# Expert stage of a hybrid block on one core: the banks are emptied by ScalarE, the expert loads move one job, the row buffers become four

## The chip, the core and the metric

The kernel runs on one core of one Trainium2 chip. The time is device microseconds of one execution, from the first to the last instruction on the core with what lies around them; less is better. PE is TensorE, ACT is ScalarE, DVE is VectorE, POOL is GpSimd, SP is SyncE, which here only issues transfers.

## The reference

One block of an encoder over 512 tokens of width 2048, all in float32. The change touches the last part of it, an expert layer (`peer`) with 128 x 128 = 16384 single-neuron experts, of which each token picks 8 x 16 = 128:

```python
def one_block(args):
    xb, eb, gb = args                      # tokens, experts picked, gates
    a = jnp.einsum("td,thkd->thk", xb, u[eb])
    act = gb * jax.nn.gelu(a)
    return jnp.einsum("thk,thkd->td", act, v[eb])
x = x + gate2 * peer(h2, ...)
```

## The kernel before

Tokens are split. 352 of them (`TD`) go through all experts densely: the U stage multiplies them with all 16384 rows of `u` (128 jobs, one 1 MB weight block each), writes the gelu of the result to memory (`gelu_scratch`), and builds the gates as a dense table (`gate_scratch`). The V stage multiplies gate times gelu with all of `v`, again 128 jobs of 1 MB. The other 160 tokens go by rows: POOL fetches for each pick the picked row of 128 tokens at once (an indirect transfer of 128 rows of 8 KB, 1 MB), and DVE takes the dot products (128 + 32 of them, `dot` and `dot_x`) and later adds the gated rows of `v` to `y_g` and `y_x` (128 + 32, `v_step`). The last 24 of `dot_x` and all of `v_step` lie in the V stage: 12 rows for every 8 jobs.

A weight job takes the same way in both stages, with two buffers at each step. SP loads `w_raw` for job n as soon as DVE is done with job n-2. ACT rounds it to `w_hi` (`hi`) once it is loaded and PE has finished job n-2. DVE subtracts to get `w_lo` (`lo`). PE multiplies 48 times (16 pieces, three products each).

In the V stage the left operand comes from `load_unit`: SP loads 4 experts of gelu (`wt`, 0.72 MB) and their gates (`gate_l`, 0.72 MB, in pieces of 512 bytes); DVE multiplies them (`weigh`), ACT rounds (`weigh_hi`), DVE subtracts (`weigh_lo`), one such unit for four jobs; PE needs it some six jobs later. `wt` and `gate_l` have one buffer each.

PE's sums of 8 jobs (a segment, 4 jobs for the first) stay in the eight PSUM banks. Then `add` scales them and adds them to `acc_o` on DVE, bank by bank, and the next segment's first matmul in a bank waits for its `added`.

The order on each engine is written out by hand in loops of 16 slots r; slot r treats weight job 6 + r (and 16 more in each turn). Slots r and r + 8 have the same form but for the half of the result, so 8 jobs are called a period here, with slots 0 to 7. SP in slot r issues the load of job 8 + r:

```python
with sp.Fori(0, 7) as i:
    for r in range(16):
        load_v(8 + r, i)
        if r % 4 == 2:
            load_unit(4 + r // 4, i)
```

DVE in slot r: `add` if r % 8 == 7, `lo`, `weigh` if r % 4 == 0, a row, `weigh_lo` if r % 4 == 1, a second row if r is even. ACT in slot r: `hi`, and behind it `weigh_hi` if r % 4 == 0. All three work strictly in order.

Of the kernel before, what the change touches and what calls it, by code (L numbers as in the profile page):

```python
# [13 lines left out]
P = 128  # L14
# [80 lines left out]
def build(nc, x_d, c_d, pos_d, prm_d, wada_d, win_d, wqr_d, wval_d, whd_d, wout_d, wwq_d, keys_d, u_d, v_d, urow_d, vrow_d, out_d):  # L95
    gelu_d = nc.dram_tensor("gelu_scratch", [NKEY, P, TD], F32).ap()
# [3 lines left out]
    with ExitStack() as ctx:  # L100
# [77 lines left out]
        e1_g = at("e1_g", 182, [P, P])  # L178
        e2_g = at("e2_g", 182.5, [P, P])
        part_g = at("part_g", 183, [P, P], U32)  # L180
        shifted_g = at("shifted_g", 183.5, [P, PH_, TOPK])
        expd_g = at("expd_g", 184, [P, PH_, TOPK])
        esum_g = at("esum_g", 184.5, [P, PH_])
        ersum_g = at("ersum_g", 184.75, [P, PH_])
        row_f = at("row_f", 185.5, [P, P])
# [9 lines left out]
        g_chunk = [at(f"g_chunk{s}", 112 + 24 * s, [P, NKEY, GC]) for s in range(2)]  # L195
        u_row = [at(f"u_row{s}", (160, 168, 192)[s], [P, D]) for s in range(3)]
        h2t = at("h2t", 0, [P, KD, T])[:, :, T - P:T]
        h2x = at("h2x", 32, [P, KD, T])[:, :, T - P:T]
        x_keep = at("x_keep", 208, [P, KD, XT])
        x_rep = at("x_rep", 192, [P, KD, P // XT, XT])  # L200
        hot2 = at("hot2", 176, [P, 2, 4, P, 2], BF16)
        hot1 = [at(f"hot1{j}", 180 + 4 * j, [P, 2, 4, P, 2], BF16) for j in range(3)]
# [7 lines left out]
        wt_hi = [at(f"wt_hi{s}", 112 + 6 * s, [P, 4, TD], F32R) for s in range(4)]  # L210
        wt_lo = [at(f"wt_lo{s}", 136 + 6 * s, [P, 4, TD], F32R) for s in range(4)]
        wt = at("wt", 176, [P, 4, TD])
        gate_l = at("gate_l", 182, [P, TD // GC, 4, GC])
# [60 lines left out]
        seg_sum, added = sem("seg_sum"), sem("added")  # L274
# [18 lines left out]
        def _(sp):  # L293
# [98 lines left out]
        def _(pool):  # L392
# [1487 lines left out]
```

## Time and profile before

| | |
|---|---|
| median of 3 runs | 3391.32 us (3388.0 to 3401.11) |
| profiled execution | 3383.77 us, span 3381.9 us |
| busy: PE / DVE / ACT / POOL | 91% / 79% / 31% / 21% |
| mean granted TensorE clock | 0.953 |
| transfers | 892.73 MB, 264 GB/s over the span |

The U stage's loop runs from about 1203 to 2200 us of the span, the V stage from 2239 us to the end. Busy shares are means over stages; a matmul's duration overlaps with its neighbour's, so a busy PE can still be slow. The granted clock is the share of 2.4 GHz (0.5 is 1.2 GHz).

### The profile page before, as it was taken

To read this page: it belongs to the slowest core of one execution; us is meant where nothing else is said; L and a number is where in the kernel's file an instruction comes from. 1 tells how busy PE (TensorE), PEld (TensorE's weight loads), DVE (VectorE), ACT (ScalarE), POOL (GpSimd) and SP (SyncE) were. 2 spreads that over 40 slices of the span, in tenths; PEclk is the share of its full clock that TensorE was granted. 3 is DMA by queue.
4 is the path that set the end of the run, shared out by engine and by line. 5 is a ranking of instruction groups with operands and counts; after the bars stand their busy time and mean duration, and the time that the engine had idled before them with its cause. 6 is when DMAs were issued, how large, how long until landed. Compare 5 with 4: busy or idle time off the path is not lost.

```text
span 3381.9 us, 44834 instructions
## 1 busy us (share of the span) xinstructions
PE 3070.1 (91%) x17253; PEld 2798.5 (83%) x17253; DVE 2673.7 (79%) x3081; ACT 1043.0 (31%) x992; POOL 724.3 (21%) x380
## 2 busy tenths in 40 slices
PE   4898978879889989999899999978999889998899
PEld 3686744447678989999899999978999889998899
DVE  6996968867773699999789999857887877877875
ACT  3323233431122334444333333222222222222221
POOL 4500000000030013233112323322332322323231
PEclk8998989879999999999999999989999999999999
DMA  8621213237734357777569999988899888898985
GB/s 349 253 100 62 83 55 128 115 122 303 292 152 174 136 195 296 298 297 297 215 219 371 357 366 371 376 333 320 334 349 343 325 347 331 339 352 315 356 336 199
DMA packets 194324, 892.73 MB, mean 264 GB/s; under 512 B 15664, under 2 KB 93616, under 8 KB 98096
## 3 DMA queue, kind: packets, MB, share of 16 engines
q1 hardware_dynamic: 123664, 491.29, 38.6%
q0 software_dynamic: 46080, 335.56, 25.8%
q10 hardware_dynamic: 24480, 64.45, 4.9%
q8 instruction: 74, 1.21, 0.1%
q14 instruction: 26, 0.21, 0.0%
HBM read 836.71 MB, written 54.53 MB: 264 GB/s over the span
## 4 chain that ended last, share of the span: by engine, by line
PE 56%; DVE 17%; DMA 17%; issue 4%; ACT 3%; POOL 2%; SPq 1%; DVEq 0%; ACTq 0%; POOLq 0%; PEldq 0%
PE bank L1459 11%; PE bank L1460 11%; PE bank L1461 11%; DMA gate_l<-gate_scratch 9%; PE bank L1793 4%; PE bank L1794 4%; PE bank L1795 4%; DMA u_row<-v_rows,urow_i 4%; DVE w_lo L830 3%; PE bank L1767 2%; ACT w_hi L452 2%; DVE ada_w L855 2%; PE bank L1670 2%; PE bank L1671 2%; PE bank L1672 2%
## 5 line engine op out<-in xcount | busy, mean ns | idle before, releaser
L452 ACT ACTIVATE w_hi<-w_raw 128x2048 fp32r<-128x2048 f32 (+1 forms) x327 | 620.2, 1897 | 1455.1 <-PE bank L1461 526.4
L830 DVE TENSOR_TENSOR w_lo<-w_raw,w_hi 128x2048 fp32r<-128x2048 f32 (+1 forms) x319 | 727.3, 2280 | 406.8 <-ACT w_hi L452 388.5
L1459 PE MATMUL bank<-act_hi,w_hi 128*128 128x352 f32 (+1 forms) x2584 | 886.9, 343 | 59.6 <-DVE w_lo L830 44.1
L1460 PE MATMUL bank<-act_lo,w_hi 128*128 128x352 f32 (+1 forms) x2584 | 877.2, 339 | 0.0
L1461 PE MATMUL bank<-act_hi,w_lo 128*128 128x352 f32 (+1 forms) x2584 | 876.5, 339 | 0.0
L1793 PE MATMUL bank<-wt_hi,w_hi 128*128 128x352 f32 x2048 | 682.2, 333 | 106.8 <-DVE acc_o L1384 65.2
L1794 PE MATMUL bank<-wt_lo,w_hi 128*128 128x352 f32 x2048 | 676.4, 330 | 0.0
L1795 PE MATMUL bank<-wt_hi,w_lo 128*128 128x352 f32 x2048 | 675.7, 330 | 0.0
L1459 PEld LDWEIGHTS bank<-act_hi,w_hi 128*128 128x128 f32 x2584 | 491.7, 190 | 94.1 <-issue 38.3
L1461 PEld LDWEIGHTS bank<-act_hi,w_lo 128*128 128x128 f32 x2584 | 491.4, 190 | 22.3
L1460 PEld LDWEIGHTS bank<-act_lo,w_hi 128*128 128x128 f32 x2584 | 492.4, 191 | 20.9 <-issue 0.2
L1793 PEld LDWEIGHTS bank<-wt_hi,w_hi 128*128 128x128 f32 x2048 | 399.5, 195 | 116.1 <-issue 69.5
L432 POOL DMA_INDIRECT u_row<-u_rows,urow_i x128 | 260.4, 2034 | 932.8 <-DVE u_row L1229 648.2
L1794 PEld LDWEIGHTS bank<-wt_lo,w_hi 128*128 128x128 f32 x2048 | 400.0, 195 | 0.0
L1795 PEld LDWEIGHTS bank<-wt_hi,w_lo 128*128 128x128 f32 x2048 | 399.0, 195 | 0.0
L432 POOL DMA_INDIRECT u_row<-v_rows,urow_i x128 | 228.4, 1784 | 519.9 <-DVE y_g L1374 505.9
L1374 DVE SCALAR_TENSOR_TENSOR y_g<-u_row,gate_g,y_g 128x2048 f32<-128x2048 f32 x128 | 300.4, 2347 | 33.5 <-DMA u_row<-v_rows,urow_i 30.7
L1229 DVE SCALAR_TENSOR_TENSOR u_row<-u_row,h2t 128x2048 f32<-128x2048 f32 x128 | 288.7, 2284 | 10.2 <-DMA u_row<-u_rows,urow_i 10.1
L421 POOL TENSOR_TENSOR act_lo<-X,act_hi 128x512 fp32r<-128x512 f32 x16 | 26.6, 1679 | 791.6 <-ACT act_hi L467 791.6
L1501 PE MATMUL bank<-act_hi,w_hi 128*128 128x512 f32 x256 | 105.1, 411 | 56.1 <-POOL act_lo L409 27.1
L1343 DVE TENSOR_TENSOR wt<-wt,gate_l 128x1408 f32<-128x1408 f32 x32 | 51.9, 1622 | 89.8 <-DMA gate_l<-gate_scratch 89.8
L1670 PE MATMUL bank<-act_hi,w_hi 128*128 128x512 f32 x256 | 107.0, 418 | 5.6 <-DVE act_lo L1116 2.9
(262 smaller groups left out, 3323.7 us busy)
## 6 DMA issues: line engine op xcount, KB each, us to landing
w_raw<-u SPq DMA_DIRECT2D x128, 1024.0 KB
w_raw<-v SPq DMA_DIRECT2D x128, 1024.0 KB
ada_w<-wada SPq DMA_DIRECT2D x80, 1024.0 KB, 5.6
w_raw<-win SPq DMA_DIRECT2D x27, 1024.0 KB
gelu_scratch<-gelu_s ACTq DMA_DIRECT2D x128, 176.0 KB
gate_scratch<-g_chunk ACTq DMA_DIRECT2D x11, 2048.0 KB, 14.2
wt<-gelu_scratch SPq DMA_DIRECT2D x32, 704.0 KB
gate_l<-gate_scratch SPq DMA_DIRECT2D x32, 704.0 KB
```

The lines of the kernel that those rows point to most:

```text
L432: pool.indirect_dma_start(u_row[n % 3][:], None, table, bass.IndirectOffsetOnAxis(ap=col, axis=0)).then_inc(u_row_loaded[n % 3], 16)
L452: act.activation(w_hi[n0 % 2][:, 0:width], w_raw[n0 % 2][:, 0:width], ACT.Copy).then_inc(hi_done, 1)
L830: dve.tensor_tensor(w_lo[s][:, 0:width], w_raw[s][:, 0:width], w_hi[s][:, 0:width].bitcast(F32), ALU.subtract).then_inc(lo_done, 1)
L1229: dve.scalar_tensor_tensor(out=row, in0=row, scalar=1.0, in1=h2t, op0=ALU.mult, op1=ALU.mult, accum_out=col).then_inc(dots_done, 1)
L1374: dve.scalar_tensor_tensor(out=y[:], in0=u_row[s % 3][:], scalar=col, in1=y[:], op0=ALU.mult, op1=ALU.add).then_inc(y_g_steps, 1)
L1459: pe.matmul(out, wh, hi_t(k), start=(k == 0), stop=False)
L1460: pe.matmul(out, wh, lo_t(k), start=False, stop=False)
L1461: last = pe.matmul(out, wl, hi_t(k), start=False, stop=(k == nk - 1))
L1670: pe.matmul(bank[s][:], wh, act_hi[:, k, :], start=(at_ == 0), stop=False)
L1793: pe.matmul(o, w_hi[s][:, col], th, start=begin is not None and e == 0, stop=False)
L1794: pe.matmul(o, w_hi[s][:, col], tl, start=False, stop=False)
L1795: last = pe.matmul(o, w_lo[s][:, col], th, start=False, stop=bool(end) and e == 1)
```

## The change

Five edits, all in or for the V stage:

1. ACT empties the banks: `evict` scales a bank into one of eight SBUF tiles `stage`; PE's next segment waits for `evicted`. DVE's `add` becomes a sum of two SBUF tiles, four in slot 0 and four in slot 1 of the next slots.
2. `load_unit` is issued at r % 4 == 1 and not 2; it still waits for the `weigh_lo` of the unit before.
3. `weigh` stands behind the two rows of its slot and not ahead of them.
4. Rows in the V stage (24 of `dot_x` and all `v_step`) use four buffers `v_row`, not three; the first waits until the first 8 of `dot_x` are done.
5. `gelu_scratch` is laid out by partition, so that `wt` is 5632 contiguous bytes per partition and not four pieces of 1408.

Buffers move to make room, `h2x` becomes contiguous, and `y_g` is cleared in the V stage's third job.

```diff
-    gelu_d = nc.dram_tensor("gelu_scratch", [NKEY, P, TD], F32).ap()
+    gelu_d = nc.dram_tensor("gelu_scratch", [P, NKEY, TD], F32).ap()
...
-                sp.dma_start(wt[:], gelu_d[rows].rearrange("e p t -> p e t")).then_inc(wt_loaded, 16)
+                sp.dma_start(wt[:], gelu_d[:, rows, :]).then_inc(wt_loaded, 16)
...
                     load_v(8 + r, i)
-                    if r % 4 == 2:
+                    if r % 4 == 1:
                         load_unit(4 + r // 4, i)
...
+                elif n >= XT - 4:
+                    pool.wait_ge(y_g_steps, m - 2)
...
+            def evict(k, half_i, turn=0):
+                for d in range(8):
+                    act.wait_ge(seg_sum, 8 * k + d + 1 + turn * 16)
+                    if k:
+                        act.wait_ge(added, 8 * (k - 1) + d + 1 + turn * 16)
+                    m = 5 * KD + 8 * half_i + d
+                    act.activation(stage[d][:], bank[d][:, 0:TD], ACT.Copy, scale=mod[:, m:m + 1]).then_inc(evicted, 1)
...
                 for r in range(16):
+                    if r % 8 == 7:
+                        evict(1 + r // 8, 1 - r // 8, i)
                     hi(J_V + 6 + r, i * 8)
                     if r % 4 == 0:
                         weigh_hi(3 + r // 4, i)
...
                 for r in range(16):
-                    if r % 8 == 7:
-                        add(1 + 2 * i0 + r // 8, 1 - r // 8, turn)
                     lo(J_V + 6 + 16 * i0 + r, turn * 8)
-                    if r % 4 == 0:
-                        weigh(3 + 4 * i0 + r // 4, turn)
+                    if r % 8 < 2:
+                        add(2 * i0 + r // 8, r // 8, r % 8, turn)
                     row(q)
                     if r % 4 == 1:
                         weigh_lo(3 + 4 * i0 + r // 4, turn)
                     if r % 2 == 0:
                         row(q + 1)
+                    if r % 4 == 0:
+                        weigh(3 + 4 * i0 + r // 4, turn)
...
-                opened = () if q == 0 else (y_ready, 1) if q == 124 else (added, 8 * (segment - 1) + 1) if r == 0 else None
+                opened = () if q == 0 else (y_ready, 1) if q == 124 else (evicted, 8 * (segment - 1) + 1) if r == 0 else None
```

SP's queue in the V loop before, from the load in slot 1 to that in slot 3 (`w_raw_54` and `w_raw_55` are the two weight buffers, and a name's number is a buffer's):

```order
L298 DMA w_raw_54<-v 128x2048
...
L298 DMA w_raw_55<-v 128x2048
...
L360 DMA wt<-gelu_scratch 128x4x352
...
L361 DMA gate_l<-gate_scratch 128x11x128
...
L298 DMA w_raw_54<-v 128x2048
```

The same place now:

```order
L301 DMA w_raw_54<-v 128x2048
...
L363 DMA wt<-gelu_scratch 128x1408
...
L364 DMA gate_l<-gate_scratch 128x11x128
...
L301 DMA w_raw_55<-v 128x2048
...
L301 DMA w_raw_54<-v 128x2048
```

The unit's two transfers have moved ahead of the load issued in slot 2, which is the weight block for slot 4 (or slot 0 of the next period).

DVE before, from the last `lo` ahead of a `weigh` through the slot after it (slots 0 and 1):

```order
L830 TENSOR_TENSOR w_lo_59<-w_raw_55,w_hi_57 128x2048
...
L1343 TENSOR_TENSOR wt<-wt,gate_l 128x1408
...
L1374 SCALAR_TENSOR_TENSOR y_g<-u_row_159,gate_g,y_g 128x2048
...
L1374 SCALAR_TENSOR_TENSOR y_g<-u_row_160,gate_g,y_g 128x2048
...
L830 TENSOR_TENSOR w_lo_58<-w_raw_54,w_hi_56 128x2048
...
L1374 SCALAR_TENSOR_TENSOR y_g<-u_row_161,gate_g,y_g 128x2048
...
L1347 TENSOR_TENSOR wt_lo_184<-wt,wt_hi_180 128x1408
```

Slots 0 and 1 now, without the second and third of four adds in each:

```order
L847 TENSOR_TENSOR w_lo_59<-w_raw_55,w_hi_57 128x2048
...
L1399 TENSOR_TENSOR acc_o<-acc_o,stage_193 128x352
...
L1399 TENSOR_TENSOR acc_o<-acc_o,stage_196 128x352
...
L1392 SCALAR_TENSOR_TENSOR y_g<-u_row_159,gate_g,y_g 128x2048
...
L1392 SCALAR_TENSOR_TENSOR y_g<-u_row_160,gate_g,y_g 128x2048
...
L1363 TENSOR_TENSOR wt<-wt,gate_l 128x1408
...
L847 TENSOR_TENSOR w_lo_58<-w_raw_54,w_hi_56 128x2048
...
L1399 TENSOR_TENSOR acc_o<-acc_o,stage_197 128x352
...
L1399 TENSOR_TENSOR acc_o<-acc_o,stage_200 128x352
...
L1392 SCALAR_TENSOR_TENSOR y_g<-u_row_161,gate_g,y_g 128x2048
...
L1367 TENSOR_TENSOR wt_lo_184<-wt,wt_hi_180 128x1408
```

Between the `lo` and the `weigh` of a slot there now stand the two rows, and in slot 0 four adds as well; in slot 4 there are no adds.

ACT now, from the `weigh_hi` of slot 4 to slot 7 (the eight `stage` rows are those of `evict`, of which the first and last stand here; before, ACT had the same rows without them):

```order
L782 ACTIVATE wt_hi_181<-wt 128x1408
...
L456 ACTIVATE w_hi_56<-w_raw_54 128x2048
...
L456 ACTIVATE w_hi_57<-w_raw_55 128x2048
...
L798 ACTIVATE stage_193<-bank,mod 128x352
...
L798 ACTIVATE stage_200<-bank,mod 128x352
...
L456 ACTIVATE w_hi_56<-w_raw_54 128x2048
```

`weigh_hi` stood and stands ahead of the next slot's `hi`; only what DVE does ahead of it has grown.

## Rows read from the trace of the kernel before

**Rows 1.** Stretches: busy us of PE, PEld, DVE, ACT, POOL; clock, DMA share, GB/s.

```profile
1203.00:2130.00 927.00, 905.15 (x6259) 897.70 (x6258) 844.92 (x1349) 369.27 (x365) 247.10 (x121) 0.99 0.80 302
2361.00:3277.00 916.00, 834.27 (x4992) 827.00 (x4991) 723.47 (x423) 233.67 (x131) 278.14 (x157) 0.96 0.89 339
```

**Rows 2.** Timeline of PE: matmuls that waited, at job 4 and in three periods.

```profile
2282.18 0.63 PE L1793 MATMUL bank<-wt_hi,w_hi 128*128 128x352 f32 x1 [7.86 <-DVE acc_o L1384]
...
2360.81 0.40 PE L1793 MATMUL bank<-wt_hi,w_hi 128*128 128x352 f32 x1 [4.75 <-DVE acc_o L1384]
...
2770.70 0.43 PE L1793 MATMUL bank<-wt_hi,w_hi 128*128 128x352 f32 x1 [2.87 <-DVE w_lo L830]
...
2783.95 0.40 PE L1793 MATMUL bank<-wt_hi,w_hi 128*128 128x352 f32 x1 [3.77 <-DVE acc_o L1384]
...
3277.35 0.63 PE L1793 MATMUL bank<-wt_hi,w_hi 128*128 128x352 f32 x1 [5.09 <-DVE acc_o L1384]
```

**Rows 3.** Timeline of ACT in the period from 2739 us.

```profile
2744.93 1.92 ACT L452 ACTIVATE w_hi<-w_raw 128x2048 fp32r<-128x2048 f32 x1 [5.72 <-PE bank L1795]
2752.57 1.91 ACT L452 ACTIVATE w_hi<-w_raw 128x2048 fp32r<-128x2048 f32 x1 [5.72 <-PE bank L1795]
2763.72 1.39 ACT L778 ACTIVATE wt_hi<-wt 128x1408 fp32r<-128x1408 f32 x1 [9.23 <-DVE wt L1343]
2765.01 1.90 ACT L452 ACTIVATE w_hi<-w_raw 128x2048 fp32r<-128x2048 f32 x1
```

**Rows 4.** Timeline of DVE in the same period.

```profile
2754.52 2.29 DVE L830 TENSOR_TENSOR w_lo<-w_raw,w_hi 128x2048 fp32r<-128x2048 f32 x1 [2.89 <-ACT w_hi L452]
2762.06 1.62 DVE L1343 TENSOR_TENSOR wt<-wt,gate_l 128x1408 f32<-128x1408 f32 x1 [5.25 <-DMA gate_l<-gate_scratch]
2763.61 4.83 DVE L1374 SCALAR_TENSOR_TENSOR y_g<-u_row,gate_g,y_g 128x2048 f32<-128x2048 f32 x2
2768.35 2.29 DVE L830 TENSOR_TENSOR w_lo<-w_raw,w_hi 128x2048 fp32r<-128x2048 f32 x1
2770.56 2.35 DVE L1374 SCALAR_TENSOR_TENSOR y_g<-u_row,gate_g,y_g 128x2048 f32<-128x2048 f32 x1
2772.82 1.62 DVE L1347 TENSOR_TENSOR wt_lo<-wt,wt_hi 128x1408 fp32r<-128x1408 f32 x1
...
2783.22 4.02 DVE L1384 SCALAR_TENSOR_TENSOR acc_o<-bank,mod,acc_o 128x352 f32<-128x352 f32 x8
```

**Rows 5.** Timeline of SP's queue: start, duration of the issue.

```profile
2742.47 0.38 SPq L360 DMA_DIRECT2D wt<-gelu_scratch  x1
2743.04 0.38 SPq L361 DMA_DIRECT2D gate_l<-gate_scratch  x1
2749.53 4.56 SPq L298 DMA_DIRECT2D w_raw<-v  x1
```

**Rows 6.** DMA queues, 2754 to 2759 us: q0 POOL's rows, q1 SP's; packets, MB, share.

```profile
q0 software_dynamic: 247, 1.88, 91.5%
q1 hardware_dynamic: 250, 0.13, 9.1%
```

**Rows 7.** DMA queues, 2783.5 to 2794 us, the whole second unit.

```profile
q1 hardware_dynamic: 2033, 2.06, 58.8%
q0 software_dynamic: 284, 2.04, 46.4%
```

**Rows 8.** DMA packets from 2739 to 2742 us, weight block and row together.

```profile
DMA packets 152, 1.23 MB, mean 410 GB/s; under 512 B 2, under 2 KB 2, under 8 KB 2
```

**Rows 9.** DMA queues, 2770.6 to 2772.9 us, then 2773.2 to 2775 us.

```profile
q0 software_dynamic: 100, 0.82, 90.7%
...
q1 hardware_dynamic: 44, 0.36, 60.8%
```

**Rows 10.** Timeline of POOL: the fetch after the pair of rows at 2763.61.

```profile
2766.22 3.03 POOL L432 DMA_INDIRECT u_row<-v_rows,urow_i x1 [13.39 <-DVE y_g L1374]
```

**Rows 11.** Timeline of DVE early in the V stage: gates waited for, in slot 0.

```profile
2304.69 1.63 DVE L1343 TENSOR_TENSOR wt<-wt,gate_l 128x1408 f32<-128x1408 f32 x1 [8.46 <-DMA gate_l<-gate_scratch]
```

More of the change, by code:

```diff
@@ L193, in build @@
         keys = at("keys", 160, [P, PH_, 2, NKEY])
[L195 to L196 removed]
+        g_chunk = [at(f"g_chunk{s}", 112 + 16 * s, [P, NKEY, GC]) for s in range(2)]
+        u_row = [at(f"u_row{s}", 164 + 8 * s, [P, D]) for s in range(3)]
         h2t = at("h2t", 0, [P, KD, T])[:, :, T - P:T]
[L198 removed]
+        h2x = at("h2x", 156, [P, KD, P])
         x_keep = at("x_keep", 208, [P, KD, XT])
[L200 to L202 removed]
+        x_rep = at("x_rep", 152, [P, KD, P // XT, XT])
+        hot2 = at("hot2", 188, [P, 2, 4, P, 2], BF16)
+        hot1 = [at(f"hot1{j}", 144 + 4 * j, [P, 2, 4, P, 2], BF16) for j in range(3)]
         gelu_s = [at(f"gelu_s{s}", 200 + 2 * s, [P, TD]) for s in range(2)]
@@ L208, in build @@
         gate_r = at("gate_r", 210, [P, TD])
[L210 to L213, printed above, removed]
+        wt_hi = [at(f"wt_hi{s}", 112 + 5.5 * s, [P, 4, TD], F32R) for s in range(4)]
+        wt_lo = [at(f"wt_lo{s}", 134 + 5.5 * s, [P, 4, TD], F32R) for s in range(4)]
+        wt = at("wt", 188, [P, 4, TD])
+        gate_l = at("gate_l", 193.5, [P, TD // GC, 4, GC])
+        v_row = u_row + [at("v_row3", 204, [P, D])]
         acc_o = at("acc_o", 0, [P, KD, T])
-        y_g = at("y_g", 204, [P, D])
         y_x = at("y_x", 32, [P, D])
+        y_g = at("y_g", 40, [P, D])
+        stage = [at(f"stage{d}", 48 + 1.375 * d, [P, TD]) for d in range(8)]
         prm = at("prm", 212, [P, NPRM])
@@ L273, in build @@
         wt_loaded, wt_ready, wth_ready, wtl_ready = (sem(n) for n in ("wt_loaded", "wt_ready", "wth_ready", "wtl_ready"))
-        seg_sum, added = sem("seg_sum"), sem("added")
+        seg_sum, evicted, added = sem("seg_sum"), sem("evicted"), sem("added")
+        v_row_loaded = [sem(f"v_row_loaded{s}") for s in range(4)]
         y_sum, x1_loaded, y_ready, out_stored = sem("y_sum"), sem("x1_loaded"), sem("y_ready"), sem("out_stored")
@@ L1315, in dot_x @@
             def dot_x(n):
-                s = P + n
-                dve.wait_ge(u_row_loaded[s % 3], 16 * (s // 3 + 1))
-                row = u_row[s % 3][:].rearrange("p (k d) -> p k d", d=P)
-                dve.scalar_tensor_tensor(out=row, in0=row, scalar=1.0, in1=h2x, op0=ALU.mult, op1=ALU.mult,
+                if n < 8:
+                    row, loaded, count = u_row[(P + n) % 3], u_row_loaded[(P + n) % 3], (P + n) // 3 + 1
+                else:
+                    row, loaded, count = v_row[n % 4], v_row_loaded[n % 4], (n - 8) // 4 + 1
+                dve.wait_ge(loaded, 16 * count)
+                r = row[:].rearrange("p (k d) -> p k d", d=P)
+                dve.scalar_tensor_tensor(out=r, in0=r, scalar=1.0, in1=h2x[:], op0=ALU.mult, op1=ALU.mult,
                                          accum_out=a_x[:, n:n + 1]).then_inc(dots_done, 1)
@@ L1396, in _ @@
             for q in range(2, 6):
-                if q == 5:
-                    dve.wait_ge(x1_loaded, 16)
-                    add(0, 0)
                 lo(J_V + q)
+                if q == 2:
+                    dve.memset(y_g[:], 0.0).then_inc(y_g_steps, 1)
+                for m in range(2):
+                    dot_x(8 + 2 * (q - 2) + m)
                 if q == 4:
                     weigh(2)
-                for m in range(2):
-                    dot_x(8 + 2 * (q - 2) + m)
                 if q == 5:
                     weigh_lo(2)
+            dve.wait_ge(x1_loaded, 16)
             def v_slots(i0, row, turn=0):
@@ L1436, in _ @@
                 lo(J_V + 118 + e)
-                if e == 0:
-                    weigh(31)
+                if e < 2:
+                    add(14, 0, e)
                 if e < 4:
@@ L1444, in _ @@
                     v_step(P + 25 + 2 * e)
+                if e == 0:
+                    weigh(31)
                 if e == 3:
```

90 lines of the change are left out of this document (43 added, 47 removed).

## Prediction

> **What bounds the kernel now.** I read the busy times by stage first [rows 1]. In the U stage PE is busy 905 of 927 us at a granted clock of 0.99: it is bound by PE. In the V stage's loop PE is busy 834 of 916 us at 0.96, DVE 723 us, and the DMA engines move 339 GB/s at a share of 0.89. So three resources are near their limit there, and none is at it.
>
> PE's timeline shows where it loses time. Between 2360.81 and 3277.35 us lie 13 periods of 8 jobs, 70.5 us each [rows 2]. A job that nothing disturbs takes 7.64 us: two starts of `w_hi` that each waited for PE alone stand 7.64 us apart [rows 3]. Eight make 61.1 us, so 9.4 us are lost per period. Two idle times make most of it, here 2.87 us for `w_lo` in slot 5 and 3.77 us for `acc_o` at the change of segment [rows 2]; the clock of 0.96 in place of 1 makes the rest, about 3 us.
>
> The timelines of DVE and ACT show what is behind both. In slot 4 DVE does `lo`, then sits 5.25 us for `gate_l` [rows 4]; ACT's `weigh_hi` waits for DVE, and the next `hi`, which is behind it, starts at 2765.01 and not at 2760.2, when PE was done with the job [rows 3]. The rows behind `weigh` are late as well, and DVE comes to `add` only at 2783.22 [rows 4].
>
> **How transfers share the engines.** This decides the forecast. From 2754 to 2759 us POOL's queue and SP's have 247 and 250 packets, 1.88 MB against 0.13 [rows 6]: they take turns packet by packet, and while a row of 8 KB packets is under way, the 512-byte packets of `gate_l` go no faster than the row's. Within SP's queue the order is strict: `w_raw`, issued at 2749.53 behind the unit, is only there for the `hi` at 2765.01, after `gate_l`, which was issued at 2743.04 and which DVE got at 2762.06 [rows 3 to 5].
>
> So I count a unit with the weight block behind it like this. From 2783.5 to 2794 us one unit went through together with 2.04 MB of rows, nearly two [rows 7]. At 410 GB/s [rows 8] a row or a weight block (1.05 MB) takes 2.6 us and these rows 5.1 us, which leaves 5.4 us of the 10.5 for the unit. The first packets come about 2.2 us after DVE's instruction ends: `lo` ended at 2770.64 and SP's queue has packets only behind 2772.9 [rows 4, 9]. For a row it is 3.5 us: the first of the pair ended near 2766, POOL spent 3.03 us from 2766.22 [rows 4, 10].
>
> **The change part by part.**
>
> *Emptying by ACT.* Eight copies of 352 columns take ACT about 0.5 us each (I take the eight adds' 4.02 us [rows 4], since DVE reads the same banks; PE needs about as long to fill them one by one). ACT stands idle in front of slot 7's `hi`, which waits for the same job, so the next segment starts at once. This removes the 3.77 us and its clock loss. The eight adds cost DVE what they cost before (0.5 each; bounds 0.4 to 0.6), but four of them now lie in slot 0 ahead of the rows.
>
> *Use behind the rows.* This makes a chain, because ACT has `weigh_hi` ahead of the next `hi`. From the start of slot 0's `hi` to the end of slot 1's `lo`: `hi` 1.9, `lo` 2.2, four adds 2.0, two rows 4.7, `weigh` 1.6, `wt_hi` 1.4, `hi` 1.9, `lo` 2.2, hand-overs 0.2 = 18.1 us [rows 3, 4]. PE has two jobs, 15.3 us, to bridge it: 2.8 us are lost though no gate is late. From slot 4 it is 16.1 us, 0.8 lost. Another 0.2 us goes in slot 2.
>
> *Loads one job sooner.* The unit is issued when `weigh_lo` is done. After slot 1's `lo` that is adds 2.0, row 2.3, `weigh_lo` 1.6 = 5.9 us, after slot 5's 3.9 us. Now the weight block of slot 4 (or 0) is behind it in SP's queue; before, that block was ahead of it, and the one behind had a job more of time. This block has to be there two PE jobs after slot 1's (or 5's) `lo`, after 15.5 (15.3) us, for PE starts on it at once.
>
> Let D be the time of unit, weight block and what rows come between: 5.4 + 2.6 us, less 0.3 for `wt` in larger pieces (0.72 MB at 410 GB/s is 1.8 us; between that and no gain), so 7.7 us + 2.6 per row. DVE takes a row about 4, 10, 13 and 17 us after slot 1's `lo`, and each is fetched again 3.5 us later; after slot 5's it is 2, 8, 11 and 15. All but the last go in full into a window that opens at 8.1 (6.1) us; I take 3.3 rows, D = 16.3. Bounds: two rows, D = 12.9; and the slower unit before, from issue to use 19.6 us [rows 4, 5], of which 2.2 are fixed, that with the block behind it less the 0.3 gives D near 19.5.
>
> So slot 4's `hi` starts 5.9 + 2.2 + 16.3 = 24.4 us after slot 1's `lo`, not 15.5, and slot 0's 3.9 + 2.2 + 16.3 = 22.4 us after slot 5's, not 15.3. A period is 24.4 + 16.1 + 22.4 + 18.1 = **81.0 us**, in general 48.4 + 2D. PE's clock adds nothing, for its starts are set by loads.
>
> The Trainium skill (DMA: Bandwidth & Descriptors, Specifications) has line rate from 512 bytes up. Here the trace speaks against it: `gate_l` and `wt` together took 5.4 us for 1.44 MB, where 410 GB/s would make 3.5. By the page a D would be 1.6 us shorter, a period 3.2, and the time some 45 us less; the sum keeps the row's 5.4.
>
> *Four row buffers.* They make rows wait less for DVE; the waits of DVE for rows are within the 5 us per period that the chains leave idle. No row is saved, so the traffic between unit and block stays. I take nothing; the bound is the 2 us at most that a row's wait costs in front of `add`, and that is gone with edit 1. The U stage has no gain to give [rows 1]; the strided store of gelu is hidden there under a DMA share of 0.80, and costs nothing up to 20% more traffic.
>
> *Start.* Early in the stage DVE waited 8.46 us for gates in slot 0 [rows 11], and that stays, since nothing of SP's order is changed there. The first segment's add no longer holds PE at job 4, where it waited 7.86 us [rows 2]; I take 7 us for it (between 0, if the late gates take it back, and the 7.86).
>
> **The sum.** From job 7 to job 119 there are 14 periods: 14 x (81.0 - 70.5) = +147, start -7: +140 us. The profiled execution took 3383.77 us (span 3381.9), so 3524 us; against the median of 3391.32, which lies 7.5 above it, **about 3530 us**.
>
> **Rivals.**
>
> *A, fewer rows between (0.12).* If only two come between unit and block, D = 12.9, the period 74.2, the time 3391 + 52 - 7 = 3436 us. For it: rows are asked for by DVE, which stands still while the block is late. Against it: three of them are taken before that. At D = 11 it is no change; that would be 1.3 rows.
>
> *B, faster (0.14).* The weight block isn't late, as slots 4 and 0 may run ahead or SP's transfers may pass one another. Then only the chains count: 61.1 + 2.8 + 0.8 + 0.2 = 64.9 us, 14 x -5.6 - 7 = -85 us: 3306 us. It decides if D stays under 7.4 (slot 4) and 9.2 (slot 0); against it is the `w_raw` that came only behind `gate_l` [rows 3 to 5], and that D without any row is 7.7.
>
> *C, PE's floor (0.03).* The chains are hidden too, 61.1 us per period: 3391 - 132 - 7 = 3252 us. The DMA engines would have to move 24 MB in it, 390 GB/s; rows show such rates only over short stretches [rows 7, 8].
>
> *D, a slower unit (0.06).* With D = 19.5 the period is 87.4, the time 3391 + 237 - 7 = 3621 us.
>
> *The change does nothing (0.03).* The wait for gates returns in the same size behind the rows, and what ACT saves goes into it: 3391 us.
>
> **How the numbers follow.** The forecast, 3460 to 3600 us, has 0.62. About 0.5% (17 us) is what a measurement of this kernel can tell from no change. Faster has B and C, 0.17; the same has 0.05 (doing nothing and the low end of A); slower 0.78. The range that leaves out no more than 2 in 10 is 3380 to 3620 us: it gives up B, C and half of D. The forecast's own range is 3460 to 3600.
>
> **What the new profile would show.** `acc_o` and `stage` no longer release PE (edit 1 right). The wait of DVE for `gate_l` is small or gone. In its place ACT's `w_hi` waits for the DMA of `w_raw` some 7 to 9 us in slots 0 and 4, 28 times, 200 us or more in all; it was held there by PE before. PE's idle time before L1793's line stands at `w_lo`, four times per period. In the DMA view the packets of 512 bytes come ahead of that weight block, with rows between. The DMA rate in the loop falls from 339 to 339 x 70.5 / 81.0, about 295 GB/s. The prediction is wrong if `w_hi` of slot 4 starts when PE ends its job two before, or if a period is shorter than 70 us; then the block was there, and the count of rows in the window, or the strict order in SP's queue, was the step that failed.

## The result, and the profile after

The changed kernel takes **3368.94 us** (median of 6 runs, 3363.03 to 3371.95), before 3386.74 (6 runs, 3384.59 to 3401.11): ratio 0.9939, 95% interval 0.9920 to 0.9958. It is 18 us faster; 3530 was forecast. The profiled execution took 3368.7 us, its span 3366.9 us.

The stretch of the V loop (same columns and same bounds as the second row of [rows 1]):

```profile
2361.00:3277.00 916.00, 841.57 (x5066) 830.37 (x5065) 725.74 (x431) 281.35 (x236) 339.51 (x158) 0.97 0.90 345
```

The rate rose from 339 to 345 GB/s; a fall to 295 was forecast. PE's timeline, where it waited: at job 4, in one period of slots, and the last of the series:

```profile
2280.26 0.63 PE L1808 MATMUL bank<-wt_hi,w_hi 128*128 128x352 f32 x1 [6.72 <-ACT stage L798]
...
2312.04 0.66 PE L1808 MATMUL bank<-wt_hi,w_hi 128*128 128x352 f32 x1 [5.67 <-DVE w_lo L847]
...
2731.72 0.66 PE L1808 MATMUL bank<-wt_hi,w_hi 128*128 128x352 f32 x1 [5.11 <-DVE w_lo L847]
2765.73 0.43 PE L1808 MATMUL bank<-wt_hi,w_hi 128*128 128x352 f32 x1 [0.87 <-DVE w_lo L847]
2803.54 0.66 PE L1808 MATMUL bank<-wt_hi,w_hi 128*128 128x352 f32 x1 [5.65 <-DVE w_lo L847]
...
3285.82 0.43 PE L1808 MATMUL bank<-wt_hi,w_hi 128*128 128x352 f32 x1 [3.15 <-DVE w_lo L847]
```

From slot 1's start at 2312.04 to that at 3285.82 are 14 periods, 69.56 us each; before 70.5 [rows 2], forecast 81.0. PE's waits at the change of segment are gone from the loop (`acc_o` released it 13 times there before, 52.2 us; now `stage` releases it 13 times for 4.0 us). In their place PE waits twice per period, at slots 1 and 5 (4.1 and 1.3 us in the mean), where the two chains end that the forecast named; it had expected four such waits. At job 4 `stage` still cost 6.72 us, where `acc_o` had cost 7.86 [rows 2]: the first segment gained 1.1 us and not 7.

ACT in the period from 2728 us: slot 4's `hi`, `wt_hi`, slot 5's `hi`, the emptying, slot 0's `hi`, `wt_hi`:

```profile
2749.61 1.91 ACT L456 ACTIVATE w_hi<-w_raw 128x2048 fp32r<-128x2048 f32 x1 [5.72 <-PE bank L1810]
2760.16 1.38 ACT L782 ACTIVATE wt_hi<-wt 128x1408 fp32r<-128x1408 f32 x1 [8.64 <-DVE wt L1363]
2761.45 1.90 ACT L456 ACTIVATE w_hi<-w_raw 128x2048 fp32r<-128x2048 f32 x1
...
2770.43 3.88 ACT L798 ACTIVATE stage<-bank,mod 128x352 f32<-128x352 f32 x8 [3.62 <-PE bank L1810]
...
2785.69 1.91 ACT L456 ACTIVATE w_hi<-w_raw 128x2048 fp32r<-128x2048 f32 x1 [9.56 <-DMA w_raw<-v]
2797.99 1.38 ACT L782 ACTIVATE wt_hi<-wt 128x1408 fp32r<-128x1408 f32 x1 [10.38 <-DVE wt L1363]
```

DVE in the same period: slot 1's `lo`, a row, slot 2's `lo`, slot 5's `lo`, and then slot 0's `weigh` and the next slot 1's `lo`:

```profile
2729.38 2.29 DVE L847 TENSOR_TENSOR w_lo<-w_raw,w_hi 128x2048 fp32r<-128x2048 f32 x1 [3.24 <-ACT w_hi L456]
...
2733.33 2.35 DVE L1392 SCALAR_TENSOR_TENSOR y_g<-u_row,gate_g,y_g 128x2048 f32<-128x2048 f32 x1
...
2737.12 2.29 DVE L847 TENSOR_TENSOR w_lo<-w_raw,w_hi 128x2048 fp32r<-128x2048 f32 x1
...
2763.38 2.29 DVE L847 TENSOR_TENSOR w_lo<-w_raw,w_hi 128x2048 fp32r<-128x2048 f32 x1 [3.25 <-ACT w_hi L456]
...
2796.33 1.62 DVE L1363 TENSOR_TENSOR wt<-wt,gate_l 128x1408 f32<-128x1408 f32 x1
2801.19 2.29 DVE L847 TENSOR_TENSOR w_lo<-w_raw,w_hi 128x2048 fp32r<-128x2048 f32 x1 [3.24 <-ACT w_hi L456]
```

This lets the forecast's four terms be read off, from the end of slot 1's `lo` at 2731.67. The last column is the mean over all 14 periods, taken from the same timelines:

| leg | forecast | in this period | mean of 14 |
|---|---|---|---|
| slot 1's `lo` to slot 4's `hi` (2749.61) | 24.4 | 17.9 | 18.0 |
| chain slot 4's `hi` to slot 5's `lo` (ends 2765.67) | 16.1 | 16.1 | 16.0 |
| slot 5's `lo` to slot 0's `hi` (2785.69) | 22.4 | 20.0 | 17.8 |
| chain slot 0's `hi` to slot 1's `lo` (ends 2803.48) | 18.1 | 17.8 | 17.8 |

Both chains are right within 0.3 us. Both legs that depend on D are not. In this period slot 4's `hi` was released by PE and not by its block, and slot 0's block was late. Over the 14 periods the block came last 9 times ahead of slot 4 and 13 times ahead of slot 0, though never by as much as forecast; the 20.0 us shown are the longest of the 14, and this period (71.8 us) is one of the two longest.

What moved in the first of these legs shows in SP's queue, in POOL's timeline and in the DMA queues (packets, MB, share) of 2738 to 2743.4 and 2743.4 to 2748.6 us:

```profile
2737.42 0.33 SPq L363 DMA_DIRECT2D wt<-gelu_scratch  x1
2738.03 0.38 SPq L364 DMA_DIRECT2D gate_l<-gate_scratch  x1
2739.58 26.59 SPq L301 DMA_DIRECT2D w_raw<-v  x4
```

```profile
2735.94 4.28 POOL L446 DMA_INDIRECT u_row<-v_rows,urow_i  x1 [9.00 <-DVE y_g L1392]
2742.23 2.74 POOL L446 DMA_INDIRECT v_row<-v_rows,urow_i  x1 [2.01 <-DVE y_g L1392]
```

```profile
q1 hardware_dynamic: 1565, 1.54, 97.0%
...
q0 software_dynamic: 165, 1.23, 56.8%
q1 hardware_dynamic: 147, 0.95, 44.5%
```

In the first stretch not one packet of a row moves: the unit has the engines alone and is through in 5.4 us. The row that DVE finished at 2735.68 has its first packet at 2743.62, 7.9 us later; the forecast took 3.5 us from [rows 4, 10]. In the second stretch the block goes through against one row.

The waits from 2313 to 3270 us (us in total, times, longest), where the forecast named them:

```profile
ACT wt_hi L782 <- DVE wt L1363: 255.3, 27, 10.4
...
ACT w_hi L456 <- DMA w_raw<-v: 154.1, 22, 9.6
...
PE bank L1808 <- DVE w_lo L847: 71.9, 28, 5.6
```

`w_hi` waits 22 times for `w_raw`, 7.0 us each, 154 us in all; 28 times of 7 to 9, 200 us or more, was forecast. That is not far off, and yet PE lost much less than forecast by it: such a wait is ACT's idle time, most of which it would have spent waiting for PE anyway (where PE was the last to release it at slot 4, the idle time was 5.7 us). DVE no longer waits for `gate_l` in this stretch (65.6 us before).

### The profile page after: what moved, and what is told of

Same layout as the page of the kernel before. It is cut to its first block, busy times and chain, and to the rows that moved or that the text cites. A ratio compares the mean times of both kernels' runs of the same rounds, so it can differ in the third digit from the quotient of the medians.

```text
span 3366.9 us, 45155 instructions
## 1 busy us (share of the span) xinstructions
PE 3063.4 (91%) x17253; PEld 2787.5 (83%) x17253; DVE 2667.0 (79%) x3081; ACT 1096.2 (33%) x1112; POOL 784.9 (23%) x380
## 4 chain that ended last, share of the span: by engine, by line
PE 50%; DVE 23%; DMA 13%; issue 8%; ACT 5%; POOL 1%; DVEq 0%; SPq 0%; ACTq 0%; PEldq 0%
PE bank L1474 11%; PE bank L1476 11%; PE bank L1475 11%; DMA w_raw<-v 8%; DVE w_lo L847 5%; ACT w_hi L456 4%; DVE y_g L1392 2%; PE bank L1782 2%; PE bank L1808 2%; DVE ada_w L872 2%; PE bank L1810 2%; PE bank L1809 2%; PE bank L1685 2%; PE bank L1686 2%; PE bank L1687 2%
## 5 line engine op out<-in xcount | busy, mean ns | idle before, releaser
L1392 DVE SCALAR_TENSOR_TENSOR y_g<-u_row,gate_g,y_g 128x2048 f32<-128x2048 f32 x96 | 225.4, 2348 | 4.1
L782 ACT ACTIVATE wt_hi<-wt 128x1408 fp32r<-128x1408 f32 x32 | 44.2, 1380 | 293.1 <-DVE wt L1363 292.7
```

Of the source, the lines that this page charges most:

```text
L1392: dve.scalar_tensor_tensor(out=y[:], in0=v_row[n % 4][:], scalar=col, in1=y[:], op0=ALU.mult, op1=ALU.add).then_inc(y_g_steps, 1)
```

## The experiments

All times are medians, each of 4 to 12 runs; ratios are to the kernel before, which ran beside them (3387.7 to 3390.2 us), with their 95% intervals. Differences below are of medians; by the ratios they come out up to 5 us otherwise. All waits are those from 2313 to 3270 us.

### Undoing one edit of the set

**e1_load_late**, edit 2 undone:

```diff
-                    if r % 4 == 1:
+                    if r % 4 == 2:
                         load_unit(4 + r // 4, i)
```

> The changed kernel with edit 2 alone undone: the unit's load again in slots 2 and 6, behind the weight block for slots 4 and 0. Late-block theory: in the changed kernel slot 0's hi waits some 5 us for its weight block behind the unit, while gates land 15 to 18 us before use; so the period of 69.6 us loses about 4 us, the time some 55 us (3315 us), and ACT's waits for w_raw fall from 154 us to under 60. Rival, the sum of transfers: the DMA engines are at a share of 0.89 whatever the order, and the time stays within 0.5%. Second rival: the gates come late again as in the kernel before, DVE waits for them, and the time rises by 10 us or more.

Measured 3395.56 us, 1.0019 (1.0009 to 1.0029). Waits of `w_hi` for `w_raw` fall from 154 to 44 us, and DVE waits 40.2 us for `gate_l` again. The second rival of the expectation holds, its theory (3315 us) does not. The forecast put a loss of 224 us on late blocks (3530 us against 3306 in rival B); in this set the early load gains 27 us.

**e2_ahead**, edit 3 undone:

```diff
                     lo(J_V + 6 + 16 * i0 + r, turn * 8)
+                    if r % 4 == 0:
+                        weigh(3 + 4 * i0 + r // 4, turn)
...
-                    if r % 4 == 0:
-                        weigh(3 + 4 * i0 + r // 4, turn)
```

> The changed kernel with edit 3 alone undone: weigh stands ahead of the adds and rows. Late-block theory with its chains: the two chains of 18 and 16 us go (2.8 + 0.8 us per period) and a late block has 3.4 us of slack; gates landed 15 us before use, so moving the use 5 to 7 us earlier makes no wait. Period near 64.5 us, the time 60 to 75 us less. Rival, the sum of transfers: within 0.5%. Rival, that the gates are what matters: a wait for gate_l of 3 us or more comes back in a slot, and the time is the same or worse.

Measured 3457.18 us, 1.0194 (1.0180 to 1.0207), where its theory had 60 to 75 us less than the changed kernel. ACT's timeline at a slot 0, and the same wait over the loop:

```profile
2757.76 1.91 ACT L456 ACTIVATE w_hi<-w_raw 128x2048 fp32r<-128x2048 f32 x1 [14.22 <-DMA w_raw<-v]
```

```profile
ACT w_hi L456 <- DMA w_raw<-v: 422.5, 44, 17.6
PE bank L1808 <- DVE w_lo L847: 138.1, 32, 9.9
```

Here is the picture that the forecast drew: the block behind the early unit comes 14 us after ACT was free for it, with 3.74 MB of rows beside 3.51 MB of SP's queue:

```profile
q1 hardware_dynamic: 1863, 3.51, 52.0%
q0 software_dynamic: 521, 3.74, 49.9%
```

(2739 to 2757 us.) So the mechanism exists, but edit 3 takes most of it away, which the forecast had as a pure cost.

One thing in it was in no forecast. The trace has 16 marks for the landing of each load. Of the block above, fifteen came by 2751.95 us and the last at 2757.66, and `w_hi` started only then. In the mean of 14 periods the last mark comes 2.4 us (slot 4) and 2.7 us (slot 0) behind the fifteenth in this kernel, at most 6.9; in the changed kernel it is 0.35 and 0.96, and 0.5 and 0.6 in f1 below. What makes one part lag, no run shows.

**e3_three**, edit 4 undone (three row buffers; the waits and counts go with them), and **e4_gelu_old**, edit 5 undone:

```diff
-        v_row = u_row + [at("v_row3", 204, [P, D])]
+        v_row = u_row
...
-    gelu_d = nc.dram_tensor("gelu_scratch", [P, NKEY, TD], F32).ap()
+    gelu_d = nc.dram_tensor("gelu_scratch", [NKEY, P, TD], F32).ap()
```

> The changed kernel with edit 4 alone undone: three row buffers in the V stage. If the fourth buffer brings rows in time, undoing it gives DVE back its waits for rows (35 us in all before) and costs 10 to 30 us. Late-block theory: chains and the late block hide such waits, and fewer rows under way let the block come sooner, so the time stays within 10 us either way.

> The changed kernel with edit 5 alone undone: gelu rows again by expert, wt in pieces of 1408 bytes. In the changed kernel a unit passes mostly with no row beside it, so by the late-block theory only the pieces' own time counts: 0.3 to 0.8 us per unit, of which only that ahead of slot 0 counts, plus 5 to 15 us in all. Rival: with a row beside it wt takes 512 turns in place of 128 and the block is 5 us later, plus 50 us or more.

Measured 3397.72 us, 1.0019 (1.0008 to 1.0030), and 3368.54 us, 0.9931 (0.9919 to 0.9943). The fourth buffer is worth 29 us and not nothing: without it DVE's `y_g` rows wait 47.9 us for their transfer (24 times), which is not among the waits of the changed kernel. Most of this (10 rows, 35 us) lies in slot 3, just ahead of slot 4's `lo`, and the chain from slot 4's `hi` to slot 5's `lo` is 18.0 us in the mean and not 16.0. The layout of gelu is worth nothing that can be measured; 5 to 15 us were expected.

**f3_add_on_dve**, edit 1 undone:

```diff
-                    if r % 8 == 7:
-                        evict(1 + r // 8, 1 - r // 8, i)
...
+                    if r % 8 == 7:
+                        add(1 + 2 * i0 + r // 8, 1 - r // 8, turn)
                     lo(J_V + 6 + 16 * i0 + r, turn * 8)
-                    if r % 8 < 2:
-                        add(2 * i0 + r // 8, r // 8, r % 8, turn)
```

> The changed kernel with edit 1 alone undone: DVE adds from the banks in slot 7 again, and ACT empties nothing. Theory (edit 1 removes a wait of 3.8 us per period, of which the rest of the set gives back little): slower than the changed kernel by 25 to 55 us, 3395 to 3425 us, with acc_o releasing PE 14 times. Rival (the chain of lo, rows and weigh sets the period, and the adds in slot 0 stand in it, 2 us): the chain is shorter without them, PE has slack, and the time is within 15 us of the changed kernel's 3369.

Measured 3361.59 us, 0.9921 (0.9904 to 0.9937): 7 us faster than with the edit by the medians, though the two intervals overlap. The rival holds: edit 1 gains nothing in this set. PE's waits:

```profile
PE bank L1808 <- DVE w_lo L843: 43.6, 27, 3.6
PE bank L1808 <- DVE acc_o L1398: 35.7, 14, 3.4
```

`acc_o` costs 35.7 us again, but the waits at the chains' ends shrink from 71.9 to 43.6 us: four adds (1.82 us) stood in slot 0's chain, which is 16.0 us without them and not 17.8. `w_hi` waits 95 us for `w_raw` and not 154.

### Fewer edits

**e5_emptying_only** is edit 1 alone, **f4_one_and_three** edits 1 and 3, **e8_ahead_late** the set without 2 and 3; the edits are those above.

> Edit 1 alone: of the changed kernel only the emptying by ACT and the adds in slots 0 and 1 remain (with the moved buffers); loads in slot 2, weigh ahead of the rows, three row buffers, gelu by expert as before. Late-block theory: PE's idle time at the change of segment (57 us over the loop) and its clock loss go, the wait for gates in slot 4 (66 us in all, 40 us at PE) stays: 40 to 70 us less than before, so less than the changed kernel too. Rival: the wait that edit 1 removes is only moved to the gates, and the time is within 0.5% of before.

> Edits 1 and 3 alone: ACT empties the banks and weigh stands behind the rows; the unit is loaded in slot 2 as before, three row buffers, gelu by expert. Theory: edit 1 alone took 3428 us, since the four adds make DVE's chain of slot 0 longer and gates are late (141 us in all); with weigh behind the rows the wait for gates goes to 40 us or less, and the time to near that of the changed kernel with edit 2 undone, plus what the fourth buffer gave (29 us): 3400 to 3440 us. Rival (edit 3 is what counts, buffers only matter with early loads): 3385 to 3400 us.

> The changed kernel with edits 2 and 3 both undone: emptying by ACT, four row buffers and gelu by partition remain. Late-block theory: the chains go and the block is ahead of the unit; gates land some 3 to 5 us later than in the changed kernel and are used 5 to 7 us sooner, so a wait for them of up to 3 us may come back in slot 4; 50 to 90 us less than the changed kernel. Rival: gates late as before, less than 20 us gained.

Measured 3427.62 us, 1.0106 (1.0087 to 1.0125); 3390.89 us, 1.0010 (0.9994 to 1.0025); and 3435.48 us, 1.0137 (1.0115 to 1.0160). Edit 1 alone makes the kernel 36 (by the ratio) to 40 us slower, where its theory had 40 to 70 us less, and e8 is 67 us slower than the changed kernel, where 50 to 90 less was expected. The wait that replaces `acc_o` is in DVE's list:

```profile
DVE wt L1363 <- DMA gate_l<-gate_scratch: 141.0, 26, 10.5
```

That is 65.6 us before, all of it in slot 4; now 79 us are in slot 4 and 62 in slot 0. The eight adds (3.6 us) now lie in slots 0 and 1, ahead of `weigh_lo`, which lets the next unit be loaded; each unit is then later. That this delay is what makes the gates late fits the place, but wasn't tried by itself. With `weigh` behind the rows (f4) the gates have time, 13.4 us of waits are left, and the loss is gone. For f4 the rival's range holds (3385 to 3400): with late loads the set without the fourth buffer and the new layout (f4) is no slower than the set with them (e1, 3395.56).

The pair e2 and e8 shows the sign of edit 2 turn: with `weigh` ahead, the early load costs 22 us (3457 against 3435), with `weigh` behind it gains 27.

### Taking the chain away

**e6_act_order** leaves all edits and puts `weigh_hi` behind the next slot's `hi` on ACT (also in the last ten jobs, not shown); **e7_act_order_late** is the same with edit 2 undone:

```diff
                     hi(J_V + 6 + r, i * 8)
-                    if r % 4 == 0:
+                    if r % 4 == 1:
                         weigh_hi(3 + r // 4, i)
```

> The changed kernel with one more edit: ACT does weigh_hi behind the hi of the next slot, so that this hi no longer waits for weigh. Late-block theory: both chains go, what stays is the late block of slot 0, of which 3.4 us are then hidden; period 64 to 65.5 us, 55 to 80 us less. Rival, the sum of transfers: within 0.5%.

> As the run before, and edit 2 undone as well: the unit behind the weight block. Late-block theory: neither chain nor late block; the floors are PE's 61.1 us per period and the transfers' sum of about 62; 62 to 64 us, 80 to 105 us less than the changed kernel. Rival, the sum of transfers already reached: no more than 0.5%.

Measured 3309.47 us, 0.9758 (0.9736 to 0.9780), and 3353.36 us, 0.9887 (0.9865 to 0.9909). This place in ACT's order is worth 59 us, within the 55 to 80 expected, and the early load 44 once it is in. For e7, 80 to 105 us less than the changed kernel were expected and 16 came: DVE waits 43.3 us for `gate_l`, and `w_hi` 316.9 us for `w_raw`. Waits in e6:

```profile
ACT w_hi L456 <- DMA w_raw<-v: 333.4, 57, 14.4
...
PE bank L1808 <- DVE w_lo L847: 39.7, 26, 5.3
```

The wait for `w_raw` doubles and PE's halves: again ACT's idle time isn't PE's loss. The late block of slot 0 stays, as expected: the leg from slot 5's `lo` to slot 0's `hi` is 20.4 us in the mean of e6.

### Holding rows back

**f1_ahead_held** is e2 with one wait more on POOL, so that the row taken in slot 1 or 5 is fetched again only when the next unit has landed; **f2_order_held** is e6 with it.

```diff
+                if n >= 14 and (n - 14) % 6 == 0 and (n - 14) // 6 < 28:
+                    pool.wait_ge(wt_loaded, 32 * (5 + (n - 14) // 6))
                 table = urow_d if m < 0 else vrow_d
```

> This is the kernel with edit 3 undone (weigh ahead of the rows), which took 3457 us, with one thing more: POOL doesn't fetch again the row that DVE takes in slot 1 (or 5) until the next unit of gelu and gates has landed. It takes away rows between the issue of a unit and the weight block behind it, and nothing else. Theory (the number of rows in the window sets the lateness of the block): rows in the window fall from about 3 to 1 or 2, the block comes 3 to 5 us sooner twice per period, w_hi's wait for w_raw falls from 422 us to under 250, and the time from 3457 to between 3340 and 3400 us. Rival 1 (the order in SP's queue alone makes the block late, rows or none): no change, 3440 to 3470 us. Rival 2: the rows held back are late for DVE in their turn and lo stands behind them: PE's wait for w_lo stays near 138 us and the time with it, while the wait for w_raw falls.

> The changed kernel with weigh_hi behind the next slot's hi on ACT (which took 3309 us), and the same hold on POOL: the row taken in slot 1 or 5 is fetched again only when the next unit has landed. Theory: there w_hi waits 333 us for w_raw, of which the row in the window makes some; with one row fewer ahead of it the block comes up to 2.6 us sooner twice per period: 3275 to 3305 us. Rival: the transfers as a whole are the bound by now (DMA share 0.93), the hold only moves a row to a later place, where it delays another block: 3300 to 3330 us.

Measured 3290.27 us, 0.9714 (0.9697 to 0.9732), and **3281.21 us**, 0.9683 (0.9666 to 0.9701), the fastest of all; f2 lies in the range of its theory, f1 below it. POOL's and ACT's timelines of f1 at the same slot 0, the queues from 2739 to 2751 us, and the loop's stretch:

```profile
2747.70 2.21 POOL L448 DMA_INDIRECT u_row<-v_rows,urow_i  x1 [14.30 <-DMA gate_l<-gate_scratch]
```

```profile
2749.49 1.91 ACT L458 ACTIVATE w_hi<-w_raw 128x2048 fp32r<-128x2048 f32 x1 [4.99 <-DMA w_raw<-v]
```

```profile
q1 hardware_dynamic: 1860, 3.61, 84.0%
q0 software_dynamic: 77, 0.50, 10.2%
```

```profile
2361.00:3277.00 916.00, 897.49 (x5563) 886.32 (x5563) 777.92 (x463) 305.88 (x249) 290.73 (x164) 1.00 0.95 363
```

The same 3.6 MB of SP's go through in 12 us and not in 18, since half a row and not 3.6 is among them; `w_hi` waits 5.0 us and not 14.2, PE is busy 98% of the loop at full clock, and the kernel is 167 us faster than e2. That is more than the 60 to 120 us that were expected; I put it down to the wait's holding back not one row but all behind it in POOL's order. The expected fall of `w_hi`'s wait for `w_raw` from 422 us to under 250 did not come (383.4 us, now in 73 waits), while PE's wait for `w_lo` fell from 138.1 to 22.1 us.

Whether the hold helps any order was still open. **g1_after_held** is the changed kernel with it, **g2_late_held** is e8 with it, **g4_before_held** the kernel before with it (there, with three buffers, at n = 13 of the same count).

> The changed kernel with the hold on POOL alone (the row taken in slot 1 or 5 is fetched again only when the next unit has landed). In the changed kernel 1 to 2 rows lie between unit and block, and the chain over weigh costs 3.6 us per period besides. Theory (rows in the window): w_hi's wait for w_raw (147 us) falls to under 60, PE's waits for w_lo stay at 2 per period from the chains: period 69.6 down to 65 to 67, 3300 to 3335 us. Rival (the chains alone set the period, the late block overlaps with them): within 15 us of 3369.

> Edits 2 and 3 undone (3435 us) with the hold. The unit is issued in slot 2, behind the weight block of slot 4. Theory: the hold shortens the unit here too (15 us to about 6 from first packet to last), the wait for gates falls from 146 us to under 40; the block behind the unit has a job more of time. So it comes near to the kernel with early loads and the hold (3290): 3270 to 3320 us, and edit 2 is worth little once rows are held. Rival (early loads are needed, the hold only makes them harmless): 3350 to 3420 us.

> The kernel before with the hold alone, one wait on POOL per four jobs. Theory (rows that are asked for while a unit is on its way slow it by 2.6 us each, in any order): the wait of DVE for gates (66 us) goes, the blocks behind it come in time, acc_o still holds PE 14 times: 3300 to 3350 us. Rival (three buffers leave DVE without rows when one is held back, up to 6 us per hold): y_g waits for rows of 60 us and more, 3380 to 3420 us.

Measured 3381.32 us, 0.9976 (0.9962 to 0.9990); 3354.20 us, 0.9900 (0.9883 to 0.9917); 3464.53 us, 1.0233 (1.0211 to 1.0254). In g1 and g2 the rivals' ranges hold, and g4 is slower still than its rival's: the hold isn't a cure for every order, and in the changed kernel it costs 12 us. In g1 `w_hi` waits only twice for `w_raw` (12.4 us), but the held rows come late in front of `weigh`, within the chain:

```profile
2402.99 2.35 DVE L1394 SCALAR_TENSOR_TENSOR y_g<-u_row,gate_g,y_g 128x2048 f32<-128x2048 f32 x1 [3.24 <-DMA u_row<-v_rows,urow_i]
2406.42 2.35 DVE L1394 SCALAR_TENSOR_TENSOR y_g<-v_row,gate_g,y_g 128x2048 f32<-128x2048 f32 x1 [1.07 <-DMA v_row<-v_rows,urow_i]
```

Where these waits are small, g1 also shows what the chains cost nearly by themselves (its mean period is 70.6 us). PE's timeline, and the stretch behind the first of its waits:

```profile
2744.20 0.58 PE L1810 MATMUL bank<-wt_hi,w_hi 128*128 128x352 f32 x1 [2.61 <-DVE w_lo L849]
2778.61 0.43 PE L1810 MATMUL bank<-wt_hi,w_hi 128*128 128x352 f32 x1 [1.97 <-DVE w_lo L849]
2812.63 0.66 PE L1810 MATMUL bank<-wt_hi,w_hi 128*128 128x352 f32 x1 [2.61 <-DVE w_lo L849]
```

```profile
2744.20:2751.00 6.80, 6.80 (x33) 6.80 (x34) 6.80 (x7) 0.00 (x0) 0.00 (x0) 0.75 0.57 181
```

That period is 68.4 us, not the 64.9 of rival B: 1.7 us of the difference is clock (0.75 over 6.8 us), for PE starts again at 1.2 GHz after the wait, for half of this stretch, and so reaches the next deadline late. In g4 DVE lacks rows, as its rival had it (the kernel before with four buffers and the hold was not run):

```profile
DVE y_g L1377 <- DMA u_row<-v_rows,urow_i: 231.9, 49, 10.6
```

In g2 the wait for gates is gone, as its theory had it (146.5 us in e8, 0.8 now), but such waits for rows are 62 us. With the hold, the early load is worth 64 us (f1 against g2).

**g3_held_add_dve** is f1 with edit 1 undone, as in f3.

> The kernel with weigh ahead and the hold (3290 us), with edit 1 undone: DVE adds from the banks in slot 7. PE there waits hardly at all (w_lo 29 us in the loop). Theory: edit 1's 3.8 us per period and the clock loss behind it come back in full, as nothing hides them: 3330 to 3370 us. Rival (the transfers set the pace there, DMA share 0.98, so PE has slack at the change of segment too): 3285 to 3305 us.

Measured 3300.72 us, 0.9747 (0.9726 to 0.9768). The rival's range holds: edit 1 is worth only 10 us even where PE waits little for `w_lo` (22.1 us in f1), since `acc_o` makes PE wait only 2.05 us each time:

```profile
PE bank L1810 <- DVE acc_o L1400: 28.7, 14, 2.6
```

### Rows in the window, counted

From the DMA packets and landing marks of the 14 periods, in the mean: us from the first packet of `wt` until the weight block behind the unit has landed in full, rows (of 1.05 MB) that moved in it, and what the forecast's form 7.7 + 2.6 per row makes of that number.

| kernel | unit after slot 1 | by the form | unit after slot 5 | by the form |
|---|---|---|---|---|
| after | 11.0 us, 1.5 rows | 11.5 | 12.7 us, 1.9 rows | 12.7 |
| e2 | 16.1, 2.8 | 14.9 | 17.4, 3.4 | 16.6 |
| e6 | 11.4, 1.6 | 11.7 | 13.9, 2.1 | 13.3 |
| f1 | 9.1, 0.2 | 8.1 | 9.5, 0.2 | 8.3 |
| g1 | 8.5, 0.0 | 7.7 | 8.7, 0.0 | 7.8 |

The rows are counted in a window whose length they help to set, so the table alone doesn't show which makes which. What shows that rows make the block late is f1 against e2, where only POOL's wait was added.

## Why the prediction was wrong

*Right: how it is built.* The period is a sum of two chains and two legs; the chains measured 17.8 and 16.0 for 18.1 and 16.1. "7.7 us + 2.6 per row" holds within 1.2 us in five kernels. `acc_o` no longer holds PE, `gate_l` no longer holds DVE.

Part of the form is luck. The 5.4 us for a unit came from [rows 7] as one unit beside 2.04 MB of rows. But SP's queue moved 2.06 MB there and a unit is 1.44: the other 0.62 MB (76 packets of 8 KB) are weight blocks, 1.5 us by the forecast's own rate, so its working should have given 3.9. A unit without rows took 5.4 us in the changed kernel all the same. By the page DMA: Bandwidth & Descriptors (Specifications) of the Trainium skill, which has line rate from 512 bytes, it would be an estimated 3.5 us; the trace disagrees, with 1.54 MB in 5.4 us, 286 GB/s, while the engines were busy 97%.

*Wrong: "I take 3.3 rows, D = 16.3".* It was 1.5 and 1.9 rows, D = 11.0 and 12.7; this is 8.9 of the 11.4 us between the forecast's period and the measured one. Rival A, with two rows, was nearest in the count and still 67 us too slow. Two things were wrong in the count. First, "each is fetched again 3.5 us later" was taken from one fetch of the kernel before, to about the end of POOL's instruction. In the changed kernel the row of slot 1 had its first packet 7.8 to 8.2 us after DVE (in all 12 periods whose rows are those of `v_step` to `y_g` or `y_x`), since POOL's own instruction took 4.28 us and the first packet came 3.2 to 3.6 us behind it; the row of slot 5 had it after 4.7 to 5.1 us. Second, the times at which DVE takes rows were laid against a window of 16 us, but the window's length itself depends on the rows in it: with the first row late, unit and part of the block are through before it, the window closes after 11 us, and what is fetched for the rows taken at 13 and 17 us falls behind it. Small shifts tip this over. How much each of the two did was not separated; f1 against e2 shows that holding rows back is worth 167 us.

*Mis-sized: "The first packets come about 2.2 us after DVE's instruction ends".* [rows 9] shows this for a load issued while a row was moving. In the changed kernel no row moves when a unit is issued, and its first packet came 0.95 us after each of 28 issues (up to 0.97), 6.7 and 4.9 us after slot 1's and slot 5's `lo`; the forecast had 8.1 and 6.1. This makes another 2.6 us per period, and 36 of the 67 us by which rival A was too slow.

With both put right the forecast's own sum comes out: 6.7 + 11.0 + 16.0 + 4.9 + 12.7 + 17.8 = 69.1 us, for the measured 69.6.

*Wrong: edit 3 as a cost only.* It was given 2.8 + 0.8 + 0.2 us per period and nothing on the other side. Undone, the kernel is 88 us slower with early loads and 40 without (e8 against e1). Behind the rows, `weigh` makes DVE stand 3.2 us before the `lo` of slots 1 and 5, and the rows of slots 0 and 4 are back before the unit is issued. That this gap is what empties the window is my reading of the timelines; the runs show only that the rows in the window fall from 2.8 and 3.4 in e2 to 1.5 and 1.9, and the times.

*Wrong: "PE's clock adds nothing".* This rested on starts set by loads. In the period shown slot 4's `hi` was released by PE (as in 5 of the 14), whose two jobs after the wait of 5.11 us took 17.9 us and not 15.3: the granted clock was 0.65 from 2731.7 to 2739 us, 2.6 us lost. Over the 14 periods, what the changed kernel loses against 61.1 us is 2.7 (slot 1 to slot 4, clock and late block together), 2.5 (the late block of slot 0) and 3.2 (the chains, 33.8 for 30.6): 8.4 of 8.5 us.

*Mis-sized: edit 1 and the buffers.* The 3.77 us removed came back: adds in the chain, later units. It is worth about -7 us in the set (not clear of noise), 10 with `weigh` ahead and the hold, and -36 to -40 alone. "I take nothing" for the fourth buffer was 29 us. For "start -7" it was 1.1 at job 4.

So the 18 us are a sum of large terms of both signs: edit 3 moves rows out of the window, which lets edit 2 gain, and both pay for edit 1 and for the chains.

## What to carry to other kernels

Before you price a load that is moved ahead of another in the same queue, find out what other queues ask for while both are on their way, and solve for window and contents together: the count is not a constant, and a share of one queue against another is only as large as what is asked for in time. A wait that an engine shows is its own idle time; price a change by where the bounding engine starts again, as e6 doubles ACT's wait and gains 59 us. And an instruction that waits for a slow partner (`weigh_hi`) goes behind the one that feeds the bounding engine; that one place in ACT's order and one wait on POOL took the kernel from 3369 to 3281 us, where the five edits together had given 18.

## What the runs showed of the hardware

A row's fetch on POOL took between 0.94 and 4.28 us. From 2313 to 3277 us of the changed kernel there are 157 fetches of rows of `v`. Of these, 27 took 0.94 us; all the others took 1.2 to 4.3 us and end 0.80 to 0.83 us behind the end of an instruction of DVE. Three of POOL's rows in the changed kernel:

```profile
2748.89 0.94 POOL L446 DMA_INDIRECT u_row<-v_rows,urow_i  x1 [1.72 <-DVE y_g L1392]
2756.38 3.03 POOL L446 DMA_INDIRECT u_row<-v_rows,urow_i  x1 [6.55 <-DVE y_g L1392]
...
2794.20 3.02 POOL L446 DMA_INDIRECT u_row<-v_rows,urow_i  x1 [11.82 <-DVE y_g L1392]
```

The first ran while DVE was idle (from 2748.62 to 2751.55). The second ended at 2759.41, DVE's row at 2758.59; the third at 2797.22, DVE's pair of rows at 2796.42; the one of 4.28 us above ended at 2740.22, DVE's `lo` (2737.12 + 2.29) at 2739.41. No run tried this by itself, so what links the two engines, and why a fetch ends behind one instruction of DVE and not an earlier one, stays open. Also, the first packet of slot 1's row comes 3.2 to 3.6 us after POOL's instruction ended, while SP's queue is full of a unit, where it was 0.7 us for the fetch of [rows 10] in the kernel before; the packet-by-packet turns of [rows 6] don't explain this. And a load is only as early as the last of its 16 parts, which in e2 came up to 6.9 us behind the fifteenth.
